# Pooling mix of a two-layer decoder on one core: averaging matrices and values split into rounded parts and remainders, seven matmuls a group in place of three in full fp32

## Chip, cores and metric

One core of a Trainium2 chip runs the whole program in one launch. The metric is the device time in microseconds; lower is better. All inputs and the output are fp32.

## What is computed

The reference is a trunk of two layers over 256 tokens of width 2048. Layer 0 mixes tokens with a gated linear recurrence and an attention; layer 1 mixes them with trailing-window means; after each mixer comes a SwiGLU network with 5632 hidden columns. The part that the change touches is layer 1's mixer:

```python
POOL_WINDOWS = (2, 4, 8, 16)
POOL_GROUP = D_MODEL // N_POOL_GROUPS

def multiscale_pool_mixer(h, w_groups, scale):
    ...
    for gi, w in enumerate(POOL_WINDOWS):
        lo = jnp.maximum(pos + 1 - w, 0)
        window_sum = prefix[:, 1:, gi] - prefix[:, lo, gi]
        count = jnp.minimum(pos + 1, w).astype(jnp.float32)
        outs.append(window_sum / count[None, :, None] - hg[:, :, gi])
    pooled = jnp.stack(outs, axis=2).astype(h.dtype)
    mixed = jnp.einsum('bsgc,gcd->bsgd', pooled, w_groups)
    return mixed.reshape(b, s, d) * scale

# in the layer loop
x = x + mix.astype(x.dtype)
h = rms_norm(x, ffn_norm[layer])
x = x + swiglu(h, ffn_w_gate[layer], ffn_w_up[layer], ffn_w_down[layer]).astype(x.dtype)
```

## The kernel before, in words

**Weights.** All weights stream through a ring of slots. A slot of `raw` holds 128 x 2048 fp32 numbers. SyncE loads it once the remainder of the slot that lay there before is made (semaphore `lo_ready`). ScalarE copies it to `hi` in the rounded type fp32r (`prepare`, line 628, "cast" below), VectorE writes the remainder raw - hi to `lo` (`prepare`, line 976, "remainder" below), and TensorE multiplies: `wide(s, ...)` does 16 matmuls against `hi` (line 1576) and 8 against `lo` (line 1582), each 512 columns wide. In the layers' feed-forward parts and in the pooling mixer the split runs three slots ahead (`AHEAD = 3`): ScalarE casts slot s + 3 when TensorE has finished slot s, which is one position of the buffer `hi[:, 0:3]`. The fourth position of `hi` and `lo` keeps sums for a later stage.

**The pooling mixer.** It has four groups g of 512 columns, one slot each. Four engines each run an order written out by hand; an instruction waits at the head of its engine's queue for its semaphores, and everything behind it on that engine waits too.

- TensorE, group g: `wide(g)` computes z = h W into bank a or b; then turn T(g-2) (eight transposes, line 1525, of the columns of x that group g-2 completed; it waits for `x_mixed`); then `mix(g-1)`. For g = 0 there is a turn of the last columns of h in their place. `mix(3)` and T(2) come after the first slot F0 of the feed-forward part, T(3) after its second slot F1; the fourth, F3, waits for the last quarter of the activations to be split.
- VectorE, group g: `keep_z(g)` (line 1334, two instructions: bank x row scale x channel scale into `zt[g % 2]`), the remainder of slot g + 3, for g > 1 `keep_x(g-2)` (line 1275: remainder of the turned columns), then `mix_in(g-1)` (line 1345: x += mix, releases `x_mixed`). For g = 0 the remainder is followed by `take_x` (line 1247, four instructions) instead. In the feed-forward part go on: remainder, `keep_x(2)`, `mix_in(3)`; remainder, `keep_x(3)`.
- ScalarE, group g: cast of slot g + 3, for g = 0 a root and the rounded part of h's last columns (`take_x`, line 786), for g > 1 `keep_x(g-2)` (line 813, four instructions, then a cast of 1024), then for g > 0 `square(g-1)` (line 800, two squares with their sums, which wait for `x_mixed`).
- GpSimd builds the averaging matrices `window` (128 x 1536 fp32) during the last group of layer 0's feed-forward part and is idle afterwards.

`mix(g)` (lines 1757 to 1766) multiplies the averaging matrices by z: three matmuls of 128 x 128 by 128 x 512, all operands fp32, two for the second 128 tokens and one for the first. Each appears in the trace as two instructions. It waits for z (`job_emptied`) and for the previous group's `mix_in` to have emptied its PSUM banks (`x_mixed`).

Of the kernel before, what the change touches and what calls it, by code (L numbers as in the profile page):

```python
# [23 lines left out]
F32 = mybir.dt.float32  # L24
F32R = mybir.dt.float32r
U32 = mybir.dt.uint32
ALU = mybir.AluOpType
# [3 lines left out]
P = 128  # L31
# [8 lines left out]
AHEAD = 3  # L40
# [7 lines left out]
GROUPS = len(WINDOWS)  # L48
# [229 lines left out]
def trunk(nc, x, mix_norm, ffn_norm, final_norm, ab_w_in, lb_logits, hg_out_norm, ab_w_out,  # L278
          pool_w, pool_scale, w_gate, w_up, w_down, out):
    with ExitStack() as ctx:  # L280
# [3 lines left out]
        def sem(name):  # L284
            return ctx.enter_context(nc.semaphore(name))
# [70 lines left out]
                  [[kept_view(2048), kept_view(3072)], [kept_view(4096), kept_view(5120)]]]  # L356
        window = work[:, 5120:6656].rearrange("p (g t) -> p g t", g=GROUPS)
        across = work[:, 3072:5120]

        main = ctx.enter_context(nc.psum_tensor("main", [P, 4, 512], F32))  # L360
        aux = ctx.enter_context(nc.psum_tensor("aux", [P, 4, 512], F32))
# [55 lines left out]
        g_ready = sem("g_ready")  # L417
        windows_made = sem("windows_made")
        mix_done = sem("mix_done")
        slot_used = sem("slot_used")  # L420
        x_T = sem("x_T")
        w_T = sem("w_T")
# [203 lines left out]
        def _(sc):  # L626
# [253 lines left out]
            for layer, groups in enumerate(LAYERS):  # L880
                norm = (N_FFN0, N_FFN1)[layer]
                if layer == 1:
                    for g in range(GROUPS):
                        prepare(S_POOL + g + AHEAD)
                        if g == 0:
                            row_root(N_MIX1)
                            take_x(T_POOL + 3, 3, V_MIX + DT)
                        else:
                            if g > 1:
                                keep_x(T_MIX + g - 2, g - 2, V_FFN + DT, 1)  # L890
                            sc.wait_ge(x_mixed, g)
                            square(N_FFN1, g - 1)
                for g in groups:
                    used = 3 * g.pair
                    if g.blocks:
                        for i in range(BLOCK):
                            prepare(g.blocks[0] + i + AHEAD)
                        for b in range(4):
                            s = g.ups[0] + b
                            if b == 3:  # L900
                                keep_up(s, g, norm)
                            prepare(s + AHEAD)
                        for i in range(BLOCK):
                            s = g.blocks[1] + i
                            if i == 0:
                                sc.wait_ge(slot_used, s + 1)
                                copy(c11, bank_x).then_inc(p1_kept, 1)
                            prepare(s + AHEAD)
                        for i in range(2):
                            prepare(g.x + i + AHEAD)  # L910
                        for b in range(4):
                            s = g.ups[1] + b
                            if b == 0:
                                sc.wait_ge(gate_ready, 4 * g.pair + 1)
                                squash(sig[:, 0, :], c11, norm, 0, used)
                            if b == 1:
                                sc.wait_ge(gate_ready, 4 * g.pair + 2)
                                squash(sig[:, 0, :], sig[:, 1, :], norm, 1, used + 1)
                            if b == 2:
                                for h in range(2):  # L920
                                    sc.wait_ge(gate_ready, 4 * g.pair + 3 + h)
                                    squash(sig[:, h, :], g_of[:, 1, h, :], norm, h, used + 2)
                            prepare(s + AHEAD)
                            if b == 2:
                                take_hidden(layer, g.unit, 0)
                    for u in g.plain:
                        for b in range(8):
                            s = u.slot + b
                            if b == 3:
                                if g.first and u.local == 0:  # L930
                                    sc.wait_ge(row_rstd, 2 * layer + 2)
                                    sc.wait_ge(a_ready, 2 * layer + 1)
                                unit_out(s, bank_a, norm, 0 if g.first else used + 3)
                            prepare(s + AHEAD)
                            if b == 0 and u.local > 0:
                                take_hidden(layer, u.unit - 1, u.local - 1)
                            if g.first and u.local == 0:
                                start_of_layer(layer, b)
                    for n, (s, m, i) in enumerate(g.down):
                        if s + AHEAD < SLOTS:  # L940
                            prepare(s + AHEAD)
                        if n == 0:
                            take_hidden(layer, g.unit + g.n - 1, g.n - 1)
                        if g.final and layer == 0 and m > 0 and i == 0:
                            take_x(T_POOL + m - 1, m - 1, V_MIX + DT)
                        if g.final and i == g.n - 1:
                            sc.wait_ge(job_emptied, g.j_down + m + 1)
                            square((N_MIX1, N_FINAL)[layer], m)
# [8 lines left out]
        def _(ve):  # L957
# [12 lines left out]
            def prepare(t):  # L970

                ve.wait_ge(hi_ready, t + 1)
                s0, i = BLOCK_OF.get(t, (t, 0))
                at = [p.at for p in PLACES[s0]]
                src = raw[:, at[SOURCE[i]], :]
                V.tensor_tensor(lo[:, split_at(t), :], src, hi[:, split_at(t), :].bitcast(F32), ALU.subtract  # L976
                                ).then_inc(lo_ready, 1)
                if t not in BLOCK_OF:
                    return

                def add(a, b):
                    V.tensor_tensor(raw[:, at[a], :], raw[:, at[a], :], raw[:, at[b], :], ALU.add  # L982
                                    ).then_inc(sum_made, 1)

                def loaded(n):
                    ve.wait_ge(raw_loaded[at[n]], 16 * PLACES[s0][n].lap)

                if i == 0:
                    loaded(1)
                    add(0, 1)  # L990
                    loaded(2)
                    add(1, 2)
                if i == 1:
                    add(0, 2)
                if i == 2:
                    loaded(3)
                    ve.wait_ge(sum_made, BLOCK_SUMS * block_index(s0) + 3)
                    add(3, 0)
# [259 lines left out]
            def take_x(k, m, gain):  # L1258
                take_lo(k, act[:, 4 * m:4 * m + 4, :, :], gain + 4 * m)
# [68 lines left out]
            def keep_z(g):  # L1328
# [9 lines left out]
                        chain.link(ins)  # L1338
                ins.then_inc(job_emptied, 1)

            def mix_in(g):

                ve.wait_ge(mix_done, g + 1)
                xs = xn[:, :, WIDE * g:WIDE * (g + 1)]
                V.tensor_tensor(xs, xs, aux[:, 0:2, :], ALU.add).then_inc(x_mixed, 1)
# [44 lines left out]
            for layer, groups in enumerate(LAYERS):  # L1390
                norm = (N_FFN0, N_FFN1)[layer]
                if layer == 1:
                    ve.wait_ge(scale_loaded, 16)
                    for g in range(GROUPS):
                        if g > 0:
                            keep_z(g)
                            prepare(S_POOL + g + AHEAD)
                            if g > 1:
                                keep_x(T_MIX + g - 2, g - 2, 1)
                            mix_in(g - 1)  # L1400
                        else:
                            sum_rows(N_MIX1)
                            invert(N_MIX1)
                            ve.wait_ge(row_rstd, N_MIX1 + 1)
                            keep_z(g)
                            prepare(S_POOL + g + AHEAD)
                            take_x(T_POOL + 3, 3, V_MIX + DT)
                for g in groups:
                    c21, e = sig[:, 1, :], g_of[:, 1, 1, :]
                    u0 = 2 * (UNIT_ALL * layer + g.unit)  # L1410
# [96 lines left out]
        def _(pe):  # L1507
# [249 lines left out]
            def mix(g):  # L1757

                if g == 0:
                    pe.wait_ge(windows_made, 2 * GROUPS)  # L1760
                pe.wait_ge(job_emptied, J_POOL + g + 1)
                need(pe, x_mixed, g)
                Z = zt[g % 2]
                mm(aux[:, 0, :], window[:, g, 0:P], Z[:, 0, :], start=True, stop=True)
                mm(aux[:, 1, :], window[:, g, 2 * P:], Z[:, 1, :], start=True, stop=False)
                mm(aux[:, 1, :], window[:, g, P:2 * P], Z[:, 0, :], start=False, stop=True).then_inc(mix_done, 1)

            for j in range(8):
                wide_job(S_OUTB + j, J_OUTB + j // 2, mid, 8 + 4 * (j % 2), j % 2 == 0, j % 2 == 1)
# [118 lines left out]
```

## Time and profile before

| | |
|---|---|
| Median of 3 runs | 1944.07 us (1942.9 to 1945.13) |
| The profiled execution's own time | 1944.98 us |
| Its span, first to last instruction | 1943.2 us |
| Mean granted TensorE clock | 0.997 of full |
| TensorE busy | 1925.4 us, 99% |
| VectorE busy | 1395.8 us, 72% |
| ScalarE busy | 924.5 us, 48% |
| GpSimd busy | 23.6 us, 1% |
| Mean DMA rate | 196 GB/s |

The profiled execution lies 0.9 us above the median, and 1.8 us of its time lies around the span. In all rows below a line that begins with a time gives the start in us from the span's start and then the length in us; lengths of grouped instructions run from the first start to the last end. Ends of matmuls are modelled, so TensorE is read by where its pieces start in the chain.

### The profile page before, as it was taken

Reading aid. Unit: us, or ns where it says so; the run is one execution under the profiler, and the core shown is the slowest. Engines: PE = TensorE matmul, PEld = TensorE weight load, DVE = VectorE, ACT = ScalarE, POOL = GpSimd, SP = SyncE. Lnnn points to the kernel's source line nnn. Section 1 sums busy time; section 2 is a strip of 40 time slices with the busy share of each in tenths; the row PEclk is TensorE's granted clock in tenths of the full one; section 3 lists DMA queues with packets and bytes.
Section 4 is the critical chain, followed back from the end, with each engine's and each line's share of the span. In section 5 each row is a group of like instructions: output and inputs, shape, how many; then the busy total and the mean of one; then the engine's idle time right before and its main releaser. Section 6 shows DMA issues by size and latency. Waiting matters only on the chain.

```text
span 1943.2 us, 21963 instructions
## 1 busy us (share of the span) xinstructions
PE 1925.4 (99%) x9268; PEld 1612.3 (83%) x9268; DVE 1395.8 (72%) x1040; ACT 924.5 (48%) x722; POOL 23.6 (1%) x85
## 2 busy tenths in 40 slices
PE   9999999999999999999999999999999999999997
PEld 7889999988888888888888887788888888888885
DVE  5656788865758868877779556756877868878754
ACT  6434434436434535545446345633544545545443
POOL 1000000000000000000000030000000000000000
PEclk9999999999999999999999999999999999999999
DMA  9555444455555654846666655464675654747751
GB/s 305 177 176 166 152 152 151 151 176 171 178 191 198 235 195 173 281 153 250 226 215 229 214 187 173 132 208 137 236 261 190 243 195 174 278 139 252 240 211 70
DMA packets 214730, 380.92 MB, mean 196 GB/s; under 512 B 5921, under 2 KB 55154, under 8 KB 214386
## 3 DMA queue, kind: packets, MB, share of 16 engines
q1 hardware_dynamic: 214560, 379.62, 57.5%
q8 instruction: 67, 1.10, 0.2%
q14 instruction: 21, 0.17, 0.0%
q10 hardware_dynamic: 82, 0.03, 0.0%
HBM read 377.53 MB, written 2.10 MB: 195 GB/s over the span
## 4 chain that ended last, share of the span: by engine, by line
PE 90%; DVE 8%; ACT 1%; issue 1%; DVEq 0%; POOL 0%; ACTq 0%; POOLq 0%
PE main L1576 39%; PE main L1582 20%; PE main L1518 8%; PE aux L1598 5%; PE main L1520 4%; DVE lo L976 4%; DVE raw L982 4%; PE aux L1602 3%; PE main L1598 2%; PE aux L1525 2%; PE main L1602 2%; PE aux L1687 1%; ACT hi L628 1%; PE main L1629 1%; PE main L1631 1%; PE main L1630 1%
## 5 line engine op out<-in xcount | busy, mean ns | idle before, releaser
L628 ACT CAST hi<-raw 128x2048 fp32r<-128x2048 f32 (+1 forms) x389 | 741.6, 1907 | 779.1 <-PE main L1582 494.1
L976 DVE TENSOR_TENSOR lo<-raw,hi 128x2048 fp32r<-128x2048 f32 x316 | 720.0, 2291 | 321.6 <-ACT hi L628 321.6
L1576 PE MATMUL main<-hi,act 128*128 128x512 f32 x1968 | 470.0, 391 | 0.0
L1576 PEld LDWEIGHTS main<-hi,act 128*128 128x128 f32 x1968 | 368.1, 188 | 77.5 <-issue 1.9
L1576 PE MATMUL main<-hi,mid 128*128 128x512 f32 x1664 | 397.0, 391 | 0.3 <-DVE mid L1243 0.3
L1576 PEld LDWEIGHTS main<-hi,mid 128*128 128x128 f32 x1664 | 310.8, 188 | 65.3 <-DVE mid L1243 1.0
L1582 PE MATMUL main<-lo,act 128*128 128x512 f32 x984 | 243.1, 389 | 0.0
L1518 PE MATMUL main<-act,hi 128*128 128x512 f32 x640 | 229.1, 401 | 0.0
L967 DVE TENSOR_TENSOR lo<-raw,hi 128x2048 fp32r<-128x2048 f32 x71 | 162.6, 2290 | 79.2 <-ACT hi L628 79.2
L1582 PEld LDWEIGHTS main<-lo,act 128*128 128x128 f32 x984 | 184.7, 188 | 38.3
L1582 PE MATMUL main<-lo,mid 128*128 128x512 f32 x832 | 205.5, 389 | 0.0
L1582 PEld LDWEIGHTS main<-lo,mid 128*128 128x128 f32 x832 | 156.2, 188 | 32.4
L1520 PE MATMUL main<-act,lo 128*128 128x256 f32 x640 | 178.9, 280 | 0.0
L982 DVE TENSOR_TENSOR raw<-raw 128x2048 f32<-128x2048 f32 x64 | 144.9, 2286 | 0.0
L1518 PEld LDWEIGHTS main<-act,hi 128*128 128x128 f32 x640 | 120.2, 188 | 28.0 <-issue 0.7
L1520 PEld LDWEIGHTS main<-act,lo 128*128 128x128 f32 x640 | 120.8, 189 | 0.9 <-issue 0.7
L1014 DVE TENSOR_TENSOR xn<-xn,main 128x1024 f32<-128x1024 f32 x48 | 58.6, 1220 | 53.3 <-PE main L1582 53.3
L1598 PE MATMUL aux<-hi,act 128*128 128x512 f32 x384 | 94.8, 389 | 0.0
L962 DVE TENSOR_TENSOR work<-work 128x256 f32<-128x256 f32 (+2 forms) x164 | 80.2, 501 | 6.4 <-PE aux L1687 1.5
L1598 PEld LDWEIGHTS aux<-hi,act 128*128 128x128 f32 x384 | 72.1, 188 | 15.0
L1602 PE MATMUL aux<-lo,act 128*128 128x512 f32 x192 | 51.3, 389 | 0.0
L628 ACT COPY work<-main 128x512 f32<-128x512 f32 x20 | 11.7, 587 | 80.1 <-PE main L1520 80.1
(169 smaller groups left out, 1287.9 us busy)
## 6 DMA issues: line engine op xcount, KB each, us to landing
raw<-in_ffn_w_gate SPq DMA_DIRECT2D x104, 1024.0 KB, 5.2
raw<-in_ffn_w_up SPq DMA_DIRECT2D x88, 1024.0 KB, 6.3
raw<-in_ffn_w_down SPq DMA_DIRECT2D x88, 1024.0 KB, 5.1
raw<-in_ab_w_in SPq DMA_DIRECT2D x55, 1024.0 KB, 5.1
raw<-in_ab_w_out SPq DMA_DIRECT2D x16, 1024.0 KB, 5.1
raw<-in_pool_w SPq DMA_DIRECT2D x4, 1024.0 KB, 5.5
xn<-in_x SPq DMA_DIRECT2D x4, 512.0 KB, 7.9
out<-xn SPq DMA_DIRECT2D x2, 768.0 KB, 4.2
```

What stands on the lines that cost most here:

```text
L628: return nc.scalar.copy(out_, in_)
L962: return V.tensor_tensor(out_, a, b, ALU.mult)
L967: V.tensor_tensor(lo[:, s.place, :], raw[:, s.place, :], hi[:, s.place, :].bitcast(F32), ALU.subtract).then_inc(lo_ready, 1)
L976: V.tensor_tensor(lo[:, split_at(t), :], src, hi[:, split_at(t), :].bitcast(F32), ALU.subtract).then_inc(lo_ready, 1)
L982: V.tensor_tensor(raw[:, at[a], :], raw[:, at[a], :], raw[:, at[b], :], ALU.add).then_inc(sum_made, 1)
L1014: V.tensor_tensor(xs, xs, bank_, ALU.add).then_inc(job_emptied, 1)
L1518: mm(bank(job)[:, c, :], hi[:, s.place, at:at + P], rhs[:, k0 + n, :, :], start=(first and n == 0), stop=False)
L1520: ins = mm(bank(job)[:, c, TOKENS:], lo[:, s.place, at:at + P], rhs[:, k0 + n, 0, :], start=False, stop=(last and n == depth - 1))
L1576: mm(o2[:, h, :], lhs[:, k0 + n, c, h * P:(h + 1) * P], w_hi, start=(first and c == 0 and n == 0), stop=False)
L1582: ins = mm(o2[:, h, :], lhs[:, k0 + n, 0, h * P:(h + 1) * P], w_lo, start=False, stop=(last and n == 3))
L1598: mm(o, a[c][:, n, :], hi[:, at, n * WIDE:(n + 1) * WIDE], start=(first and c == 0 and n == 0), stop=False)
L1602: ins = mm(o, a[0][:, n, :], lo[:, at, n * WIDE:(n + 1) * WIDE], start=False, stop=(last and n == 3))
```

## The change

Before the first group ScalarE copies all four averaging matrices to `window_hi` (fp32r, in the free position of `hi`) and VectorE writes the remainder of those applied to the first 128 tokens to `window_lo`. In every group ScalarE copies z to a rounded half and VectorE subtracts it from z to give the other half, in two areas of `mid`. `mix(g)` then does seven fp32r matmuls of 512 columns and waits for VectorE's half (`z_lo`, a new semaphore) in place of `job_emptied`. The remainder of the other averaging matrices is not used.

```diff
--- before.py
+++ after.py
@@ -356,6 +356,10 @@
                   [[kept_view(2048), kept_view(3072)], [kept_view(4096), kept_view(5120)]]]
         window = work[:, 5120:6656].rearrange("p (g t) -> p g t", g=GROUPS)
         across = work[:, 3072:5120]
+        window_hi = hi[:, AHEAD, 0:GROUPS * 3 * P].rearrange("p (g t) -> p g t", g=GROUPS)
+        window_lo = lo[:, AHEAD, 0:GROUPS * P].rearrange("p (g t) -> p g t", g=GROUPS)
+        z_halves = [mid[:, 4 * n:4 * n + 4, :, :].rearrange("p k c t -> p (k c t)")
+                    .rearrange("p (c h d) -> p c h d", c=2, h=2) for n in range(2)]
 
         main = ctx.enter_context(nc.psum_tensor("main", [P, 4, 512], F32))
         aux = ctx.enter_context(nc.psum_tensor("aux", [P, 4, 512], F32))
@@ -417,6 +421,9 @@
         g_ready = sem("g_ready")
         windows_made = sem("windows_made")
         mix_done = sem("mix_done")
+        window_split = sem("window_split")
+        z_hi = sem("z_hi")
+        z_lo = sem("z_lo")
         slot_used = sem("slot_used")
         x_T = sem("x_T")
         w_T = sem("w_T")
@@ -885,7 +892,11 @@
                         if g == 0:
                             row_root(N_MIX1)
                             take_x(T_POOL + 3, 3, V_MIX + DT)
-                        else:
+                            sc.wait_ge(windows_made, 2 * GROUPS)
+                            copy(window_hi, window).then_inc(window_split, 1)
+                        sc.wait_ge(job_emptied, J_POOL + g + 1)
+                        copy(z_halves[g % 2][:, 0], zt[g % 2]).then_inc(z_hi, 1)
+                        if g > 0:
                             if g > 1:
                                 keep_x(T_MIX + g - 2, g - 2, V_FFN + DT, 1)
                             sc.wait_ge(x_mixed, g)
@@ -1338,6 +1349,12 @@
                         chain.link(ins)
                 ins.then_inc(job_emptied, 1)
 
+            def split_z(g):
+
+                ve.wait_ge(z_hi, g + 1)
+                Z = z_halves[g % 2]
+                V.tensor_tensor(Z[:, 1], zt[g % 2], Z[:, 0].bitcast(F32), ALU.subtract).then_inc(z_lo, 1)
+
             def mix_in(g):
 
                 ve.wait_ge(mix_done, g + 1)
@@ -1395,6 +1412,7 @@
                         if g > 0:
                             keep_z(g)
                             prepare(S_POOL + g + AHEAD)
+                            split_z(g)
                             if g > 1:
                                 keep_x(T_MIX + g - 2, g - 2, 1)
                             mix_in(g - 1)
@@ -1405,6 +1423,10 @@
                             keep_z(g)
                             prepare(S_POOL + g + AHEAD)
                             take_x(T_POOL + 3, 3, V_MIX + DT)
+                            ve.wait_ge(window_split, 1)
+                            V.tensor_tensor(window_lo, window[:, :, 0:P], window_hi[:, :, 0:P].bitcast(F32),
+                                            ALU.subtract).then_inc(window_split, 1)
+                            split_z(g)
                 for g in groups:
                     c21, e = sig[:, 1, :], g_of[:, 1, 1, :]
                     u0 = 2 * (UNIT_ALL * layer + g.unit)
@@ -1757,13 +1779,17 @@
             def mix(g):
 
                 if g == 0:
-                    pe.wait_ge(windows_made, 2 * GROUPS)
-                pe.wait_ge(job_emptied, J_POOL + g + 1)
+                    pe.wait_ge(window_split, 2)
+                pe.wait_ge(z_lo, g + 1)
                 need(pe, x_mixed, g)
-                Z = zt[g % 2]
-                mm(aux[:, 0, :], window[:, g, 0:P], Z[:, 0, :], start=True, stop=True)
-                mm(aux[:, 1, :], window[:, g, 2 * P:], Z[:, 1, :], start=True, stop=False)
-                mm(aux[:, 1, :], window[:, g, P:2 * P], Z[:, 0, :], start=False, stop=True).then_inc(mix_done, 1)
+                Z = z_halves[g % 2]
+                mm(aux[:, 0, :], window_hi[:, g, 0:P], Z[:, 0, 0, :], start=True, stop=False)
+                mm(aux[:, 0, :], window_hi[:, g, 0:P], Z[:, 1, 0, :], start=False, stop=False)
+                mm(aux[:, 0, :], window_lo[:, g, :], Z[:, 0, 0, :], start=False, stop=True)
+                for c in range(2):
+                    mm(aux[:, 1, :], window_hi[:, g, 2 * P:], Z[:, c, 1, :], start=(c == 0), stop=False)
+                    ins = mm(aux[:, 1, :], window_hi[:, g, P:2 * P], Z[:, c, 0, :], start=False, stop=(c == 1))
+                ins.then_inc(mix_done, 1)
 
             for j in range(8):
                 wide_job(S_OUTB + j, J_OUTB + j // 2, mid, 8 + 4 * (j % 2), j % 2 == 0, j % 2 == 1)
```

## Rows read from the trace of the kernel before

**Rows 1.** The page: busy time of TensorE, and the chain's shares by engine.

```profile
PE 1925.4 (99%) x9268; PEld 1612.3 (83%) x9268; DVE 1395.8 (72%) x1040; ACT 924.5 (48%) x722; POOL 23.6 (1%) x85
PE 90%; DVE 8%; ACT 1%; issue 1%; DVEq 0%; POOL 0%; ACTq 0%; POOLq 0%
```

**Rows 2.** The chain in order of time around the mixer: start, length, what.

```profile
1190.91 3.64 PE main L1576 x16
...
1196.37 0.86 PE aux L1764 x2
...
1198.94 3.65 PE main L1576 x16
...
1204.42 0.87 PE aux L1525 x8
...
1237.53 3.63 PE main L1576 x16
```

**Rows 3.** The timeline of ScalarE and VectorE, groups 0 and 1: start, length, what.

```profile
1193.55 1.55 ACT L786 ACTIVATE act<-aux,vecs 128x256 fp32r<-128x256 f32 x4
...
1193.88 1.41 DVE L1334 SCALAR_TENSOR_TENSOR work<-main,norms,work 128x512 f32<-128x512 f32 x2
...
1195.20 2.28 DVE L976 TENSOR_TENSOR lo<-raw,hi 128x2048 fp32r<-128x2048 f32 x1
...
1196.46 1.90 ACT L628 CAST hi<-raw 128x2048 fp32r<-128x2048 f32 x1 [1.36 <-PE main L1582]
...
1197.40 1.66 DVE L1247 SCALAR_TENSOR_TENSOR act<-aux,vecs,act 128x256 fp32r<-128x256 f32 x4
...
1198.97 1.40 DVE L1334 SCALAR_TENSOR_TENSOR work<-main,norms,work 128x512 f32<-128x512 f32 x2
...
1202.49 1.22 DVE L1345 TENSOR_TENSOR xn<-xn,aux 128x1024 f32<-128x1024 f32 x1
```

**Rows 4.** The timeline, a subtraction of 128 x 512 on VectorE.

```profile
1237.52 2.85 DVE L1283 TENSOR_TENSOR work<-work 128x512 f32<-128x512 f32 x4
```

**Rows 5.** The timeline from one mix_in to the next, groups 2 and 3.

```profile
1210.73 1.22 DVE L1345 TENSOR_TENSOR xn<-xn,aux 128x1024 f32<-128x1024 f32 x1
...
1211.98 0.63 ACT L800 ACTIVATE rows_in<-xn 128x512 bf16<-128x512 f32 x1 [2.42 <-DVE xn L1345]
...
1213.44 1.90 ACT L628 CAST hi<-raw 128x2048 fp32r<-128x2048 f32 x1
...
1215.24 1.56 ACT L813 ACTIVATE work<-aux,vecs 128x256 f32<-128x256 f32 x4
...
1215.37 2.29 DVE L976 TENSOR_TENSOR lo<-raw,hi 128x2048 fp32r<-128x2048 f32 x1 [0.58 <-ACT hi L628]
...
1216.84 1.05 ACT L628 CAST act<-work 128x1024 fp32r<-128x1024 f32 x1
...
1217.92 1.22 DVE L1275 TENSOR_TENSOR act<-work,act 128x1024 fp32r<-128x1024 f32 x1 [0.26 <-ACT act L628]
1219.07 1.21 DVE L1345 TENSOR_TENSOR xn<-xn,aux 128x1024 f32<-128x1024 f32 x1
```

**Rows 6.** Waits by engine and releaser: total, times, longest.

```profile
PE main L1614 <- DVE lo L1026: 1.9, 1, 1.9
```

**Rows 7.** Windows: stretch, its length, busy PE, PEld, DVE, ACT, POOL; granted clock; DMA.

```profile
8.00:12.00 4.00, 1.58 (x11) 1.34 (x12) 3.35 (x7) 4.00 (x10) 1.58 (x5) 1.00 1.05 398
12.00:16.00 4.00, 4.00 (x14) 3.10 (x13) 3.71 (x5) 2.59 (x3) 0.00 (x0) 0.64 1.05 385
16.00:20.00 4.00, 4.00 (x23) 3.45 (x22) 2.48 (x5) 2.87 (x5) 0.00 (x0) 0.94 1.05 385
...
1932.00:1936.00 4.00, 0.00 (x0) 0.00 (x0) 1.61 (x4) 3.71 (x7) 0.00 (x0) 0.85 0.00 0
```

**Rows 8.** The chain where it leaves TensorE, layer 1's first block stage.

```profile
1340.89 1.83 PE main L1582 x8
1342.79 1.92 ACT hi L628
```

## The prediction

> **What bounds the kernel now.** I read the page first. TensorE is busy for 99% of the span and carries 90% of the chain [rows 1], so at first sight every microsecond taken from it is a microsecond won. The chain in order of time shows the stretch of the change: slots, turns and mixes stand end to end on TensorE. A slot takes 5.46 us (16 and 8 matmuls, 1190.91 to 1196.37), a mix 2.57 us (1196.37 to 1198.94), and the slot behind it ends when the next turn starts, at 1204.42 [rows 2]. Nothing stands between them, so VectorE and ScalarE are hidden there now. The question is by how much, because the change gives both of them work between a slot and its mix. For that I read the timeline of the two engines [rows 3, 5].
>
> **TensorE's own saving.** A matmul of 512 columns in the rounded type takes 3.64 / 16 = 0.227 us; a full fp32 one takes 0.86, and three make the 2.57 us [rows 2]. Seven rounded ones: 7 x 0.227 = 1.59 us. Saved: 0.98 us a group, 3.9 us for four.
>
> Between back-to-back instructions of VectorE or ScalarE the next starts 0.08 to 0.1 us before the record of the last one ends (VectorE: 1195.20 + 2.28 against 1197.40); after a release it takes 0.03 to 0.1 us more [rows 3, 5]. I use the start-to-start times.
>
> **Step 1, the first mix is held up.** In group 0 VectorE runs keep_z from 1193.88, the slot's remainder from 1195.20, take_x from 1197.40, and is through at 1198.97 [rows 3]. Behind these, in its written order, come the two new subtractions. The remainder of the matrices is 128 x 512: 2.85 / 4 = 0.71 us by the subtraction of that size [rows 4]; I take 0.6, start to start, and keep 0.75 as the upper end. The remainder of z is 128 x 1024, 1.22 us by the same operation in keep_x [rows 5]. So z_lo comes at 1198.97 + 0.6 + 1.22 = 1200.8. ScalarE's half is hidden: take_x ends at 1195.10 [rows 3]; the copy of 1536 columns lies between a cast of 1024 (1.05) and one of 2048 (1.90) [rows 5], at 1.48, and ends at 1196.5; the copy of z adds 1.05, to 1197.5, before VectorE asks for it. The next slot's cast moves from 1196.46 to 1197.4, which its remainder, now after 1202, does not feel. TensorE, ready at 1196.37, idles 4.4 us and runs the mix until 1202.4; before, it was done at 1198.94. Queued behind the held mix is slot 2, which now ends at 1207.9, not 1204.42: 3.5 us late.
>
> **Step 2, VectorE behind.** After the first z_lo it runs keep_z(1) from 1200.7 (before 1198.97), 1.32 us, the slot's remainder, 2.2, the second new subtraction, 1.14, and mix_in(0), 1.22. That ends at 1206.6; before it ended at 1202.49 + 1.22 = 1203.7 [rows 3]. Mix(0) is done at 1202.4, so it is not what mix_in waits for.
>
> **Step 3, a loop that was just covered.** mix_in(g-1) releases the squares on ScalarE, and behind these in its queue stand the next cast, the products of keep_x and their cast; they release keep_x's remainder on VectorE and the next mix_in behind it. The rows give 0.04 + 1.46 (squares) + 1.80 (cast) + 1.60 (products) + 1.08 (cast) + 1.15 (remainder) + 1.21 (mix_in) = 8.34 us [rows 5]. TensorE's group is 5.46 + 0.87 + 2.57 = 8.9 us, longer, so the loop is hidden now. The change puts the copy of z between cast and products: 1.05 less the overlap, 0.97. The loop becomes 9.3 us, while TensorE's group falls to 5.46 + 0.87 + 1.59 = 7.9. The other branch, through VectorE's new subtraction (cast, 2.2, 1.14), reaches keep_x 0.2 us sooner than ScalarE's, and so is no longer. The loop thus takes over: mix_in(1) ends at 1206.6 + 9.3 = 1215.9, mix_in(2) at 1225.2, and mix_in(3), whose round has no z left to split, 8.34 later at 1233.55.
>
> TensorE meanwhile: T(0) and mix(1) until 1210.35, slot 3 until 1215.8; T(1) waits for mix_in(1), 0.15 us; mix(2) until 1218.4, F0 until 1223.9; T(2) waits for mix_in(2), 1.4 us; mix(3) until 1227.75, F1 until 1233.2; T(3) waits for mix_in(3), 0.4; F2 until 1239.95. F3 needs keep_x(3), at 1233.55 + 0.04 + 1.46 + 1.80 + 1.60 + 1.08 + 1.22 = 1240.75, and waits another 0.9 us. It starts at 1240.8, before at 1237.53 [rows 2]: **3.3 us late.** As a sum: holds 4.4 + 0.15 + 1.4 + 0.4 + 0.9 = 7.25, less 3.9 saved. The error in the four late holds is that of some twenty row durations; I allow 1 us either way.
>
> **Step 4, the clock.** The trace of before never stops TensorE in mid-run for 4.4 us, so this is bounded by the nearest rows. Its longest wait is 1.9 us, early in the span [rows 6], in the stretch 8 to 12 us, where it was busy for 1.58 of 4 us at the full 2.4 GHz. Right behind, the granted clock is 0.64 and then 0.94 of full: 0.36 x 2 x 4 + 0.06 x 2 x 4 = 3.4 us at 1.2 GHz, though TensorE was busy throughout, so 1.7 us of work lost. After its last matmul too the clock drops, within 6 us of idleness (0.85 in 1932 to 1936) [rows 7]. Bounds of the cost here: nothing, and two such stretches, 3.4 us. I take one, 1.7 us, since the hold is longer than the one that was followed by a drop. About 0.2 us is absorbed: slot 2 ends at 1207.9, but the cast that it releases is held by the squares until 1208.06 anyway. Cost: 1.5 us. The Trainium skill (TensorE: Matmul & The Clock Gate, Part 1) says that the default state is the throttled one and that activity releases it; by that rule a TensorE that stands still comes back at the lower clock. Without that rule the sum would be 3.3, with it 4.8.
>
> **What costs nothing.** The new slots of `hi` and `lo` are free then, no copy waits for them. GpSimd's matrices are made in the layer before. SyncE's queue gets no new instruction; its loads follow the remainders, which come up to 4 us later, but are needed three slots after. Beyond F3 the stretch until the first block stage is TensorE's, and where the chain then leaves it, it is for a cast that starts 0.07 us after a slot ends (1340.89 + 1.83 to 1342.79) [rows 8]. All that follows hangs on TensorE and moves with it: nothing is made up later.
>
> **Sum.** 3.3 + 1.5 = 4.8 us on one execution: 1944.98 becomes 1949.8; against the median of the runs, which is 0.9 us lower, 1944.07 + 4.8 = **1948.9 us**.
>
> **The rivals.**
> (a) *Holds as above, clock stays at 2.4 GHz*: +3.3, 1947.4. For it: the only drop in mid-run came where several waits lay close together. Against it: the hold is more than twice the longest seen.
> (b) *Only the first hold counts* and the loop is covered, because ScalarE copies z while it would wait anyway: 4.4 - 3.9 = +0.5, and +2.2 with the clock: 1944.6 to 1946.3. Against it: the squares come late in ScalarE's order, and between them and keep_x no idle time is left in the rows.
> (c) *Faster.* The split is hidden and TensorE's saving stands whole: 1944.07 - 3.9 = 1940.1. Its place is group 0: it holds if VectorE has z_lo by 1196.4. It would have to do 2.2 + 1.57 + 0.6 + 1.22 us of work between 1195.20 and 1196.4. It decides if those instructions run in another order than written, or if the split comes before the remainder of the slot. Nothing in the rows speaks for it.
> (d) *The change does not do what it says*: a rounded matmul on these operands runs at the fp32 price, 7 x 0.86 = 6.0 us a group, +3.45 x 4 = 13.8, 1957.9 or more. Against it: all 0.227 us rows are of that type.
>
> **How the numbers follow.** Forecast 0.62, (a) 0.20, (b) 0.12, (c) 0.05, (d) 0.01. A measurement of this kernel can tell about 0.2%, 3.9 us, from no change. The forecast's own range, from 0.8 to 3.4 us for the clock and 1 us for the loop, is 1947.4 to 1951.2. With (a) and the upper part of (b), and the 1 us by which the runs of before scatter, the range is 1945.6 to 1951.2. Slower by over 0.2%: four fifths of the forecast, a third of (a), and (d): 0.58. Within: 0.37. Faster: 0.05.
>
> **What would show it.** In the changed trace mix(0) starts near 1200.9 and VectorE's 1024-wide subtraction ends just before it; the seven matmuls of mix(1) take 1.6 us; mix_in follows mix_in after 9.3 us in groups 2 and 3; T(2) starts some 1.4 us after F0 ends; F3 starts 3 to 5 us later than before; the granted clock shows a stretch near 0.5 right after 1200. The forecast is wrong if mix(0) starts before 1199, if T(2) or F3 follows its predecessor at once, or if a shift seen at F3 is gone at the first block stage.

## The result and the profile after

The changed kernel takes 1949.30 us (median of 9 runs, 1948.65 to 1951.26), the kernel before 1944.07 us (9 runs beside them): 5.2 us more, a ratio of 1.0028 with a 95% interval of 1.0019 to 1.0037. A second set of 7 runs, described below, gives 1949.45 against 1943.71, 1.0028 again. It is slower by a little more than the 0.2% that such a measurement can tell from no change. Forecast were 1948.9 us and a range of 1945.6 to 1951.2.

The page of the changed kernel answers to [rows 1]:

```profile
span 1948.6 us, 21981 instructions
PE 1924.6 (99%) x9272; PEld 1614.0 (83%) x9272; DVE 1400.8 (72%) x1045; ACT 930.2 (48%) x727; POOL 23.7 (1%) x85
PE 88%; DVE 8%; ACT 2%; issue 1%; DVEq 0%; POOL 0%; ACTq 0%; POOLq 0%
```

TensorE's busy time fell by only 0.8 us, less than the 3.9 us that its matmuls save, in part because some of the new ones ran at half the clock (below). VectorE has 5.0 us more work and ScalarE 5.7. None of that explains 5.2 us while both stand still for a quarter of the time or more; the place in the two queues does.

The timeline of the changed kernel in group 0 (start, length, engine, line, tiles, in brackets the idle time before), against [rows 3]:

```profile
1193.58 1.41 DVE L1345 SCALAR_TENSOR_TENSOR work<-main,norms,work 128x512 f32<-128x512 f32 x2
...
1194.68 1.49 ACT L635 CAST hi<-work 128x1536 fp32r<-128x1536 f32 x1
1194.90 2.28 DVE L987 TENSOR_TENSOR lo<-raw,hi 128x2048 fp32r<-128x2048 f32 x1
1196.05 1.06 ACT L635 CAST mid<-work 128x1024 fp32r<-128x1024 f32 x1
...
1197.10 1.65 DVE L1258 SCALAR_TENSOR_TENSOR act<-aux,vecs,act 128x256 fp32r<-128x256 f32 x4
...
1198.67 0.68 DVE L1427 TENSOR_TENSOR lo<-work,hi 128x512 fp32r<-128x512 f32 x1
1199.27 1.22 DVE L1356 TENSOR_TENSOR mid<-work,mid 128x1024 fp32r<-128x1024 f32 x1
...
1200.64 0.47 PE L1786 MATMUL aux<-mid,hi 128*128 128x512 f32 x1 [4.58 <-DVE mid L1356]
...
1203.43 4.31 PE L1598 MATMUL main<-hi,act 128*128 128x512 f32 x16
```

VectorE works without a gap from 1193.58 to 1200.49. Its new subtractions stand last in that row of work, and TensorE idles for 4.58 us in front of its first mix. ScalarE's halves were ready at 1197.1. The mix then takes 2.8 us, not 1.6, and the start of the next slot is stretched too. The windows of the same execution say why (stretch, length, busy PE, PEld, DVE, ACT, POOL, granted clock, DMA share, GB/s):

```profile
1198.00:1200.00 2.00, 0.00 (x0) 0.00 (x0) 2.00 (x4) 0.91 (x1) 0.00 (x0) 1.00 0.74 189
1200.00:1202.00 2.00, 1.36 (x4) 1.16 (x5) 2.00 (x4) 0.15 (x1) 0.00 (x0) 0.75 0.86 335
1202.00:1204.00 2.00, 2.00 (x6) 1.52 (x6) 2.00 (x2) 0.89 (x1) 0.00 (x0) 0.50 0.01 4
1204.00:1206.00 2.00, 2.00 (x10) 1.60 (x9) 2.00 (x3) 0.00 (x0) 0.00 (x0) 0.89 0.36 54
```

Twice the missing share gives the time at 1.2 GHz: (0.25 + 0.50 + 0.11) x 2 x 2 = 3.4 us.

From one mix_in to the next, groups 2 and 3, against [rows 5]:

```profile
1216.23 1.21 DVE L1362 TENSOR_TENSOR xn<-xn,aux 128x1024 f32<-128x1024 f32 x1
1217.48 0.63 ACT L807 ACTIVATE rows_in<-xn 128x512 bf16<-128x512 f32 x1 [2.42 <-DVE xn L1362]
...
1218.87 1.90 ACT L635 CAST hi<-raw 128x2048 fp32r<-128x2048 f32 x1
...
1220.66 1.05 ACT L635 CAST mid<-work 128x1024 fp32r<-128x1024 f32 x1
...
1221.61 1.56 ACT L820 ACTIVATE work<-aux,vecs 128x256 f32<-128x256 f32 x4
...
1223.19 1.05 ACT L635 CAST act<-work 128x1024 fp32r<-128x1024 f32 x1
...
1224.28 1.23 DVE L1286 TENSOR_TENSOR act<-work,act 128x1024 fp32r<-128x1024 f32 x1
1225.42 1.22 DVE L1362 TENSOR_TENSOR xn<-xn,aux 128x1024 f32<-128x1024 f32 x1
```

The round takes 1225.42 - 1216.23 = 9.19 us, with the copy of z (1220.66) in the middle of it, and every step starts at the latest 0.05 us after the one before it has ended. TensorE now waits for this round. Its weight loads, which come just ahead of the matmuls, show it best (waits of the stretch 1190 to 1245: total, times, longest):

```profile
PEld aux L1547 <- DVE xn L1362: 2.4, 3, 1.4
PEld main L1598 <- DVE act L1286: 1.0, 1, 1.0
```

Three turns wait for mix_in and F3 waits for keep_x(3). A weight load already waits while the matmul before it still runs, so these 3.4 us are more than TensorE loses by them: from slot 3 to F4 it takes 35.76 us here and 33.23 in e7 below, where no turn waits, which makes 2.5 us.

**A ruler for the experiments.** The intervals of the ratios are about 0.0009 either way, 1.7 us, and executions already differ by up to 2.9 us before the mixer (last section). So I also use the trace: the time from the start of slot 1 to the start of F5, the sixth slot of the feed-forward part, which is never held in any kernel here. Before (the two ends of it in the timeline):

```profile
1190.67 3.89 PE L1576 MATMUL main<-hi,act 128*128 128x512 f32 x16
...
1248.24 3.79 PE L1576 MATMUL main<-hi,act 128*128 128x512 f32 x16
```

and after:

```profile
1190.36 3.89 PE L1598 MATMUL main<-hi,act 128*128 128x512 f32 x16
...
1253.09 3.79 PE L1598 MATMUL main<-hi,act 128*128 128x512 f32 x16
```

57.57 and 62.73 us: 5.16 us arise here. The spans differ by 5.4 us; slot 1 starts 0.3 us earlier in the changed kernel, so another 0.5 to 0.6 us arises behind F5. It is one place near 1569, in the third block group of layer 1, which I did not follow up; in a second profile of the changed kernel (e11) nothing is added behind F5.

### The profile page after: what moved, and what is told of

Its sections match the earlier page's. It is cut to its first block, busy times and chain, and to the rows that moved or that the text cites. A ratio compares the mean times of both kernels' runs of the same rounds, so it can differ in the third digit from the quotient of the medians.

```text
span 1948.6 us, 21981 instructions
## 1 busy us (share of the span) xinstructions
PE 1924.6 (99%) x9272; PEld 1614.0 (83%) x9272; DVE 1400.8 (72%) x1045; ACT 930.2 (48%) x727; POOL 23.7 (1%) x85
## 4 chain that ended last, share of the span: by engine, by line
PE 88%; DVE 8%; ACT 2%; issue 1%; DVEq 0%; POOL 0%; ACTq 0%; POOLq 0%
PE main L1598 38%; PE main L1604 19%; PE main L1540 8%; PE aux L1620 5%; PE main L1542 4%; DVE lo L987 4%; DVE raw L993 4%; PE aux L1624 3%; PE main L1620 2%; PE main L1624 2%; PE aux L1547 2%; ACT hi L635 1%; PE aux L1709 1%; PE main L1651 1%; PE main L1653 1%; PE main L1652 1%
```

## The experiments

Eleven kernels, each timed in five rounds beside the kernel before. "Trace" is the change of the ruler against 57.57 us, in one execution.

| Kernel | Median, us | Before, us | Ratio (95% interval) | Trace |
|---|---|---|---|---|
| e1 seven matmuls only | 1941.92 | 1943.83 | 0.9991 (0.9982 to 1.0000) | -1.60 |
| e2 split only | 1947.57 | 1943.83 | 1.0020 (1.0011 to 1.0029) | +4.14 |
| e3 hold filled | 1946.43 | 1943.83 | 1.0015 (1.0006 to 1.0024) | +3.50 |
| e4 mix_in first | 1946.90 | 1943.83 | 1.0016 (1.0007 to 1.0025) | +3.15 |
| e5 squares late | 1947.19 | 1944.04 | 1.0016 (1.0007 to 1.0025) | +3.74 |
| e6 z sooner | 1945.92 | 1944.04 | 1.0010 (1.0001 to 1.0019) | +2.59 |
| e7 all moves | 1942.54 | 1944.04 | 0.9993 (0.9984 to 1.0002) | -1.19 |
| e8 all moves, filled | 1941.94 | 1944.04 | 0.9990 (0.9981 to 0.9999) | -1.12 |
| e9 filled, squares late | 1944.64 | 1943.71 | 1.0005 (0.9996 to 1.0014) | +1.11 |
| e10 seven, squares late | 1939.86 | 1943.71 | 0.9981 (0.9972 to 0.9990) | -3.41 |
| e11 changed, again | 1949.45 | 1943.71 | 1.0028 (1.0017 to 1.0039) | +6.15 |

### e1: the seven matmuls alone

The kernel before, with the new operand views and this edit. The split is left out and the operands are whatever lies there, so the kernel doesn't compute the layer; it only has the timing of the seven matmuls.

```diff
-                Z = zt[g % 2]
-                mm(aux[:, 0, :], window[:, g, 0:P], Z[:, 0, :], start=True, stop=True)
...
+                Z = z_halves[g % 2]
+                mm(aux[:, 0, :], window_hi[:, g, 0:P], Z[:, 0, 0, :], start=True, stop=False)
+                mm(aux[:, 0, :], window_hi[:, g, 0:P], Z[:, 1, 0, :], start=False, stop=False)
...
```

> Seven rounded matmuls a group with the waits and the order of before; nothing is split, the operands are what lies in those areas, so the splitting of z and of the matrices is left out. Theory of the loop (mix_in to mix_in 8.34 us through ScalarE and VectorE, TensorE's group 7.9): mix(0) starts at 1196.4, T(0) to T(3) each wait 0.3 to 0.4 us for mix_in, F3 waits 0.9 us, and only about 1.5 us of the 3.9 comes out: 1942.5. Rival, TensorE's saving stands whole when nothing is split: no waits at T(g), 1940.1.

Measured: 1.9 us faster (the interval reaches up to no difference), 1.60 in the trace. The waits, and two mix_in in a row:

```profile
PEld aux L1530 <- DVE xn L1350: 2.3, 4, 0.8
```

```profile
1209.34 1.22 DVE L1350 TENSOR_TENSOR xn<-xn,aux 128x1024 f32<-128x1024 f32 x1
...
1217.59 1.21 DVE L1350 TENSOR_TENSOR xn<-xn,aux 128x1024 f32<-128x1024 f32 x1
```

The round of 8.25 us is what [rows 5] gave, and with TensorE at 7.9 us a group it binds. Even with a free split, half of the saving or more would have been lost in this order of work.

### e2: the split alone

The changed kernel with the mix and the waits of before.

```diff
-                    pe.wait_ge(window_split, 2)
-                pe.wait_ge(z_lo, g + 1)
+                    pe.wait_ge(windows_made, 2 * GROUPS)
+                pe.wait_ge(job_emptied, J_POOL + g + 1)
...
-                Z = z_halves[g % 2]
+                Z = zt[g % 2]
...
```

> All copies and subtractions of the changed kernel, but the mix is the full fp32 one of before with its waits, so nothing waits for the split. Theory that VectorE's queue and the loop are the price: mix(0) starts at 1196.4 at once, T(0) waits 2.2 us for mix_in(0), T(1) and T(2) 0.4 each, F3 0.3: +3.3 us, 1947.4, with the clock at full speed all through. Rival (b), only the hold of the first mix counts: no change, 1944.1. If each engine's work simply hid behind TensorE it would be 1944.1 too.

Measured: 3.7 us slower, 4.14 in the trace. T(0) is held as forecast:

```profile
PEld aux L1547 <- DVE xn L1362: 2.6, 1, 2.6
```

But the clock did not stay up (windows, columns as above):

```profile
1204.00:1206.00 2.00, 1.22 (x6) 1.22 (x7) 2.00 (x3) 1.21 (x3) 0.00 (x0) 0.71 0.84 288
1206.00:1208.00 2.00, 2.00 (x6) 1.21 (x5) 0.05 (x1) 2.00 (x4) 0.00 (x0) 0.50 0.56 216
```

TensorE itself stood still for 2.2 us in front of T(0) and was then slow for (0.29 + 0.50 + 0.06) x 4 = 3.4 us, 1.7 us of work lost. With the restart (0.3 us, worked out from e7 below) these two come to 4.2, so they account for the 4.14. The forecast of 3.3 had no drop and had late holds of 1.1 us in its place, and none of those appeared: that it came within 1 us is in part luck. Whether they would show without the drop no run tells, so e2 shows the delay through VectorE's queue and says nothing of the loop. What stands is that the splitting costs 3.7 us though nothing waits for its results, because its instructions delay mix_in(0) behind them in the queue. It is not enough to ask who waits for a new result.

### e3: the hold filled

```diff
+                    for n in range(18):
+                        mm(aux[:, 0, 0:P], ones[:], ones[:], start=True, stop=True)
                     pe.wait_ge(window_split, 2)
```

> The changed kernel with 18 matmuls of 128 x 128 ones put before the waits of mix(0), 18 x 0.215 = 3.9 us at 2.4 GHz, so that TensorE works through most of the 4.5 us hold. Theory of the clock: no stretch at 1.2 GHz after 1200, F3 some 1.5 us earlier than in the changed kernel, 1947.8. Rival, the slow stretch costs nothing because the loop sets the pace anyway: 1949.3.

Measured: 1946.43 us, 2.6 above before; 3.50 in the trace, 1.66 less than the changed kernel. The granted clock is 1.00 in every window of 2 us from 1196 to 1210. The loop stays as it was:

```profile
PEld aux L1547 <- DVE xn L1362: 2.4, 3, 1.5
```

The theory of the clock holds: the same waits and the same work, without the drop, cost 1.7 us less in the trace and between 2.6 and 3.1 by the medians.

### e4 and e5: the loop opened at either end

e4, on VectorE:

```diff
                             prepare(S_POOL + g + AHEAD)
+                            mix_in(g - 1)
                             split_z(g)
                             if g > 1:
                                 keep_x(T_MIX + g - 2, g - 2, 1)
-                            mix_in(g - 1)
```

> The changed kernel with one edit of VectorE's order: mix_in(g-1) ahead of the subtraction of z and of keep_x, right behind the slot's remainder. Theory of the loop: it is opened, since mix_in no longer stands behind ScalarE's copy and products; no waits at T(1), T(2), T(3) and F3; only the first hold and the slow clock are left, 4.5 - 3.9 + 1.5 to 1.7 = +2.2, 1946.3. Rival, the loop is not what costs (the late holds come from TensorE's own shift): 1949.3 as the changed kernel.

e5, on ScalarE (with the same shift by one group in the first two slots behind the mixer):

```diff
                             if g > 1:
                                 keep_x(T_MIX + g - 2, g - 2, V_FFN + DT, 1)
-                            sc.wait_ge(x_mixed, g)
-                            square(N_FFN1, g - 1)
+                                square(N_FFN1, g - 2)
```

> The changed kernel with one edit of ScalarE's order: the squares of a group run one group later, behind the next keep_x, so that the cast no longer stands behind a wait for mix_in. Theory of the loop: opened at its other end, so the holds at T(1), T(2), T(3) and F3 go, as they did when mix_in was moved on VectorE; the first hold and the slow clock stay: +2.3 us against before with 1.7 us of work lost to the clock, up to +3 with 2.2: 1946.1 to 1946.8. Rival, moving mix_in helped because VectorE's queue was shortened ahead of the turn, and ScalarE's order does not matter: as the changed kernel, 1948.7.

Measured: 3.1 and 3.15 us above before, 3.15 and 3.74 in the trace. In e4 no turn waits for mix_in any more, in e5 two wait 0.6 us together; F3 waits 0.3 in e4. e4 is 0.9 us above its figure, e5 a little above its upper one. The granted clock of e4:

```profile
1196.00:1198.00 2.00, 0.00 (x0) 0.00 (x0) 2.00 (x6) 1.88 (x2) 0.00 (x0) 0.75 0.26 36
1198.00:1200.00 2.00, 0.39 (x1) 0.42 (x2) 2.00 (x3) 0.00 (x0) 0.00 (x0) 0.50 0.92 342
1200.00:1202.00 2.00, 2.00 (x6) 1.52 (x6) 2.00 (x3) 1.05 (x1) 0.00 (x0) 0.50 0.40 151
1202.00:1204.00 2.00, 2.00 (x7) 1.58 (x6) 2.00 (x2) 0.00 (x0) 0.00 (x0) 0.54 0.00 0
```

That is a slow stretch of 6.8 us, a good third of it while TensorE stood still; the part in which it worked took some 2.1 us of work from it. In e5 it was 6.8 us too, but TensorE worked through most of it and lost some 2.8. That and the restart are why both lie above their figures. These two runs thus mix two causes; e9 keeps them apart.

### e6: a shorter first hold, the loop left closed

```diff
-                            take_x(T_POOL + 3, 3, V_MIX + DT)
-                            ve.wait_ge(window_split, 1)
-                            V.tensor_tensor(window_lo, window[:, :, 0:P], window_hi[:, :, 0:P].bitcast(F32),
-                                            ALU.subtract).then_inc(window_split, 1)
                             split_z(g)
+                            take_x(T_POOL + 3, 3, V_MIX + DT)
```

and the split of the matrices moved into the last down projection of layer 0.

> The changed kernel with the matrices split during layer 0's last group and the subtraction of z ahead of take_x on VectorE, so that z_lo(0) comes 2.2 us sooner and the first hold shrinks from 4.5 to 2.3 us; the loop stays closed. Theory: mix_in(0) is still set by VectorE's queue, and the loop runs from there, so late holds of 0.3, 1.4, 1.4, 0.4 and 0.9 us show up and the 2.2 us come out only in part: +2.7 us, 1946.5, whether the clock drops or not, because TensorE then waits less at T(0) and T(1). Rival (b), only the first hold counts: 2.2 us less than the changed kernel and no clock drop, +0.9, 1944.7.

Measured: 1.9 us above before, 2.59 in the trace; the clock stayed at 1.00 this time. The waits:

```profile
PEld aux L1549 <- DVE xn L1363: 3.8, 4, 1.5
PE aux L1788 <- DVE mid L1357: 2.4, 1, 2.4
```

The first hold fell by 2.2 us and the waits at the turns rose from 2.4 to 3.8. Against e3, which has no drop either, the trace gives 0.9 us, not 2.2: 1.3 of the 2.2 us came back further down. Rival (b) of the prediction, that only the first hold counts, asked for +0.9; the trace has 2.59. By the medians alone the two would not be told apart well (1.9, interval 0.2 to 3.7).

### e7 and e8: all moves, and the hold filled

e7 joins e4, e5 and e6. e8 adds 9 matmuls of ones ahead of the first mix, as in e3.

> All moves together: matrices split early, z ahead of take_x, mix_in ahead of the other subtractions, squares a group later. Theory: one hold of 2.2 us at mix(0) is all that is left, 2.2 - 3.9 = -1.7 us, 1942.1, if the clock stays up; with a slow stretch after the hold -0.1, 1943.7. Rival, the split has a cost of its own that no order removes (it is work on two engines that are 72% and 48% busy): slower than before, above 1944.

> The same with 9 matmuls of 128 x 128 ones ahead of the wait of mix(0), 1.9 us at 2.4 GHz, inside the hold of 2.2 us. Theory of the clock: no stretch at 1.2 GHz after 1190, and the time is -1.7 us against before, 1942.1, whatever the kernel without them does. Rival, a hold of 2.2 us does not lower the clock and the filling changes nothing: both kernels equal.

Measured: -1.5 us (unclear by its interval) and -2.1 us (just outside it); -1.19 and -1.12 in the trace. In e7 this is the one wait that is left on TensorE in the stretch:

```profile
PE aux L1789 <- DVE mid L1358: 2.4, 1, 2.4
```

The clock stayed up in both, so they say nothing of how it drops: the rival of e8, that the filling changes nothing, is what was seen, though e2 shows that a hold of this length can be followed by a drop. The rival of e7, slower than before in any order, falls. In this order the split hides, except for the 2.4 us before the first mix, and no run shows an order that removes those too. The two kernels are equal within their scatter; e8 is the only version with the full computation whose interval lies below 1, by 0.0001 and as one of eleven kernels, so it is the traces of both that carry the gain of 1.2 us.

### e9: the loop by itself

e3 with the squares of e5.

> The kernel with the filled hold, and the squares a group later: against the filled kernel it differs in the loop alone, with the clock out of play in both. Theory of the loop: only the first hold is left, 4.5 + 0.3 for the restart - 3.9 = +0.9 us against before, 1944.9, and in the trace no hold at T(1), T(2), T(3), F3. Rival, the late holds are not the loop's: as the filled kernel, 1946.4 or +3.3 in the trace.

Measured: 1944.64 us, 0.9 above before, no difference that can be told; 1.11 in the trace. Against e3 that is 1.7 us by the medians, each taken against the kernel before beside it (less than their intervals together can tell from nothing), and 2.39 in the trace, with no matmul waiting for mix_in any more. What is left of waits for mix_in in the stretch:

```profile
PEld aux L1548 <- DVE xn L1363: 0.6, 2, 0.4
```

### e10: TensorE's saving set free

e1 with the squares of e5.

> The seven matmuls alone (nothing is split, the splitting of z and of the matrices is left out), and the squares a group later. Theory: in the run of the seven matmuls alone the loop of 8.34 us kept back 2 us; with it opened nearly all of TensorE's saving comes out, -3.7 us, 1940.3. Rival, the other 2 us are lost on TensorE itself (the switch between kinds of matmul, or the longer chain of seven into two banks): still 1941.9.

Measured: 3.85 us faster, interval 0.9972 to 0.9990; 3.41 in the trace. By the medians the whole 3.9 us is there, in the trace all but 0.5. One wait of 0.8 us at T(0) remains (0.4 on the matmuls), since mix_in(0) still stands behind a remainder on VectorE.

### e11: the changed kernel again

> The changed kernel once more, beside the others on one chip. The hold of 4.6 us at mix(0) and the holds at T(2), T(3), F3 as before within 0.1 us. Open is the slow stretch: 3.4 us in the changed kernel's profile, 6.8 in two of the experiments with the same hold. If it varies from execution to execution: 3.4 or 6.8 here, 1949.3 within 1 us. Rival, its length belongs to the kernel: 3.4 again.

Measured: 5.7 us above before. The holds are the same (4.6 at the mix, 2.4 at three turns, 1.0 at F3), the slow stretch is not:

```profile
1198.00:1200.00 2.00, 0.00 (x0) 0.00 (x0) 2.00 (x4) 0.47 (x1) 0.00 (x0) 0.75 0.89 251
1200.00:1202.00 2.00, 1.80 (x4) 1.49 (x5) 2.00 (x4) 0.59 (x1) 0.00 (x0) 0.50 0.67 259
1202.00:1204.00 2.00, 2.00 (x6) 1.56 (x5) 2.00 (x2) 0.46 (x1) 0.00 (x0) 0.50 0.01 4
1204.00:1206.00 2.00, 2.00 (x6) 1.54 (x6) 1.84 (x2) 0.12 (x1) 0.00 (x0) 0.55 0.48 98
```

(0.25 + 0.50 + 0.50 + 0.45) x 4 = 6.8 us, and the trace gives +6.15, not +5.16. The length is a matter of the execution, not of the kernel. Held against this execution, whose slow stretch is as long as theirs, e5 is 2.41 us and e4 3.00 us shorter in the trace: the loop once more, this time with the drop on both sides (e4 lost some 0.7 us less to the clock).

## Why the prediction was right, and where it was off

**The sum.** The trace divides the 5.16 us into three parts: e9 has the first hold less TensorE's saving, 1.11; e3 less e9 is the loop, 2.39; the changed kernel less e3 is the clock, 1.66. The prediction had 4.4 - 3.9 = 0.5, then 2.85, then 1.5: 4.8. All three mechanisms were there. The first part was 0.6 us too small, the loop 0.4 to 0.5 too large and the clock too small, by 0.2 us in this execution and by some 1.1 where the slow stretch is the long one. Errors in both directions partly cancelled, so that 1948.9 came within 0.4 us of 1949.3 is in part luck; the medians could not tell such a distance anyway. The prediction's own range isn't the plain sum of the bounds that it names either: 0.8 to 3.4 us for the clock and 1 us for the loop give 1947.2 to 1951.8, not 1947.4 to 1951.2. The measured time lies inside both.

**TensorE's saving.** Forecast 0.98 us a group. In e7 a group takes 7.94 us (1199.21 to 1207.15), in the kernel before 8.93: 0.99. e10 shows it in the time (3.85 us by the medians, 3.41 in the trace). The Trainium skill (FP8 and Floating Point Precision, TensorE Precision Notes) says that true fp32 takes four passes through the array. The rows come near it, 0.86 us against 0.227, 3.8 times as much.

**Step 1, the first hold.** Forecast 4.4, measured 4.58. The remainder of the matrices took the 0.6 us assumed, ScalarE's copy of 1536 columns 1.49 (forecast 1.48). What the step left out is the restart: in e7, at full clock, slot 2 starts 9.77 us after slot 1, where a slot (5.44), the wait (2.40) and the mix (1.6) make 9.44, so 0.3 us go beyond the wait. With the 0.2 us that the hold was longer, that is most of the 0.6 us by which this part was too small.

**Steps 2 and 3, the loop.** Forecast 9.3, 9.3 and 8.34 us from mix_in to mix_in; measured 11.17, 9.19 and 8.25. In the first of these rounds ScalarE's cast waits 1.86 us for TensorE to finish slot 2, which the drop of the clock had made late. In e3, without the drop, 9.55, 9.18 and 8.25. The copy of z adds 0.94 us. The late holds were forecast at 2.85 us and cost 2.5 (35.76 against 33.23 us from slot 3 to F4; the weight loads' waits of 2.4 and 1.0 us overlap matmuls), which fits the 2.39 between e3 and e9. The prediction said that the loop was covered by little before the change, 8.34 under 8.9; e1 shows it from the other side, since there it binds with nothing added to it.

**Step 4, the clock.** Forecast 1.5 us between 0 and 3.4; 1.66 in the profiled execution. It can cost more: of the four executions traced with the hold of 4.6 us, three (e4, e5, e11) had the long stretch of 6.8 us, and the medians put the difference between the changed kernel and e3 at 2.6 to 3.1 us. This term was sized too small: one slow stretch was taken as the likeliest, and in these traces the double one is the more frequent. What decides between the two lengths stays open. The Trainium skill (TensorE: Matmul & The Clock Gate, Part 1) has the lower clock as the default and activity as what releases it. The runs agree so far: every drop near the mixer comes during a hold or within half a microsecond of its end, the full clock is back 3.4 or 6.8 us later, and with the hold of e3 filled by matmuls whose results nobody uses it stayed at 1.00. Which holds are followed by a drop they do not settle (last section).

**The rivals.** (a), no drop: shown wrong by the windows of both profiles of the changed kernel; its figure of +3.3 is close to what e3 gives with the drop prevented (3.50 in the trace). (b), only the first hold: refuted by e6, by the 2.39 us between e3 and e9, and by the waits. (c), faster: TensorE's part of it is real (e10), but it needs results 4.5 us sooner than VectorE has them. (d) has no support, at full clock the new matmuls follow each other after 0.23 us.

**"Nothing is made up later"** held: the changed kernel is 4.85 us later at the start of F5 and 4.83 at the cast behind the first block stage that [rows 8] show (1347.62 against 1342.79); 5.4 at the end of the span.

## What to carry to other kernels

An engine that is busy for 99% may be covering a round through the others that is only a little shorter than its own; before speeding it up, time that round from the trace (here 8.3 us under 8.9), because here it took over at once (e1). Price new work on a "hidden" engine by its place in the queue: what stands behind it and who waits for that, even if nobody waits for the new result itself. Where a wait stands in the middle of a queue (the squares, mix_in), moving it to where it holds nothing else up decides here whether the saving comes out at all.

## What was not expected of the hardware

- **Slow stretches have two lengths here**: 3.4 us (the changed kernel's first profile, e2, and the early one of the kernel before) and 6.8 us (e4, e5, e11). In e4 the clock fell before 1198, while TensorE was still idle and less than 3 us after the hold began. In the changed kernel's first profile it fell only when the hold of 4.6 us was over (1.00 in 1198 to 1200, 0.75 in 1200 to 1202). So both the moment of the drop and its length differ between executions.
- **Holds near 2 us may or may not be followed by a drop**: one did at 2.2 us (e2), those of 2.4 us in e6 and e7 did not.
- **The same thing happens at the start of the program**: the granted clock of the stretch 12 to 20 us is 0.79 to 0.85 in five profiles (before, changed, e6, e8, e11), where slot 1 starts between 1189.9 and 1191.3, and 1.00 in the other eight, where it starts between 1188.4 and 1189.4. So some 1.5 us of the scatter between runs is made long before the mixer, and a distance inside the trace tells differences that medians blur.
- **A restart after a hold** costs TensorE about 0.3 us beyond the wait (9.77 against 9.44 us in e7).
